# A five-branch recurrent decoder layer on one core: start, attention, C heads, S5 taps and output reordered

## What is computed

```python
h = rmsnorm(x, norm_pre)
p = split_cols(h @ w_in)                       # 2048 -> columns of the five branches
oa = s5_branch(p["a_x"], ...)                  # complex diagonal recurrence, then GLU
ob = hgrn2_branch(p["b_q"], p["b_f"], p["b_i"], ...)
oc = gla_branch(p["c_q"], p["c_k"], p["c_v"], p["c_r"], ...)   # 4 heads, values 256 wide
od = rglru_branch(p["d_x"], ...)               # width-4 conv, gated recurrence
oe = mem_attend(p["e_q"], mem_k, mem_v)        # 4 heads over 256 memory tokens
branches = stack([oa * silu(p["a_g"]), ..., oe * silu(p["e_g"])])
pb = einsum("ntcw,cwd->ntcd", branches, w_branch)
merged = einsum("ntcd,ntcd->ntd", sigmoid(h @ w_merge), pb)
y = x + rmsnorm(merged @ w_out, norm_post)
```

## Time and profile before

| | us |
|---|---|
| median of 3 runs (lowest, highest) | 2093.11 (2087.61, 2093.49) |
| the profiled execution | 2093.22 |
| its span in the trace | 2091.40 |
| TensorE busy (matmul) | 1990.5, 95% |
| TensorE weight loads busy | 1906.4, 91% |
| VectorE / ScalarE / GpSimd busy | 1278.6 / 906.3 / 411.4 |
| granted clock, mean over the span | 0.974 |

### The profile page before, as it was taken

The page is one execution under the profiler, slowest core; times in us unless marked ns, Lnnn a source line. Parts: engine busy times, 40 slices in busy tenths (PEclk is TensorE's granted clock), DMA queues, the critical chain, the costliest instruction groups (busy, mean ns, idle before and its releaser), DMA issues.

```text
span 2091.4 us, 36635 instructions
## 1 busy us (share of the span) xinstructions
PE 1990.5 (95%) x15254; PEld 1906.4 (91%) x15254; DVE 1278.6 (61%) x2092; ACT 906.3 (43%) x1307; POOL 411.4 (20%) x708
## 2 busy tenths in 40 slices
PE   6999986999999999999999999999999999999995
PEld 5889986999998989898999999999999999999994
DVE  6654437777665656565777777777565565554543
ACT  4533433444553434343555555545333333433342
POOL 3678877875000000000000000000100000000000
PEclk9999998999998989898999999999999999999997
DMA  6766754555443434444444444444655444555441
GB/s 237 256 245 243 264 181 134 174 182 187 157 159 134 160 136 151 145 149 159 139 143 153 141 150 144 147 140 137 219 165 191 161 155 149 193 178 165 151 162 66
DMA packets 91222, 350.46 MB, mean 168 GB/s; under 512 B 11728, under 2 KB 11872, under 8 KB 87472
## 3 DMA queue, kind: packets, MB, share of 16 engines
q1 hardware_dynamic: 76032, 278.17, 40.3%
q0 software_dynamic: 12144, 49.85, 6.7%
q10 hardware_dynamic: 2880, 20.09, 2.5%
HBM read 321.15 MB, written 26.92 MB: 166 GB/s over the span
## 4 chain that ended last, share of the span: by engine, by line
PE 58%; DVE 7%; ACT 4%; issue 3%; DMA 0%; POOL 0%; ACTq 0%; DVEq 0%
PE ps L1581 57%; DVE w_lo L1034 2%; DVE g_X L1028 1%; DVE g_X L1034 1%; ACT g_t L566 1%; ACT w_hi L566 1%; ACT L566 1%; DVE g_X L1037 0%; ACT g_X L566 0%; DMA a_h<-in_a_h 0%; DVE g_b L1439 0%; PE ps L1869 0%; DVE acc L1031 0%; DVE acc L1028 0%; DVE g_k L1034 0%
## 5 line engine op out<-in xcount | busy, mean ns | idle before, releaser
L1581 PE MATMUL ps<-h_hi,w_hi 128*128 128x288 f32 x2960 | 892.9, 302 | 39.6 <-DVE w_lo L1034 22.9
L1034 DVE TENSOR_TENSOR w_lo<-raw,w_hi 128x1024 fp32r<-128x1024 f32 x522 | 649.6, 1255 | 439.5 <-ACT w_hi L566 436.0
L1581 PE MATMUL ps<-h_hi,w_lo 128*128 128x288 f32 x2960 | 877.8, 297 | 0.0
L1581 PE MATMUL ps<-h_lo,w_hi 128*128 128x288 f32 x2960 | 875.4, 296 | 0.0
L566 ACT ACTIVATE w_hi<-raw 128x1024 fp32r<-128x1024 f32 x522 | 547.3, 1056 | 655.3 <-PE ps L1581 646.9
L1581 PEld LDWEIGHTS ps<-h_hi,w_hi 128*128 128x128 f32 x2960 | 559.7, 189 | 60.6 <-issue 43.0
L1581 PEld LDWEIGHTS ps<-h_hi,w_lo 128*128 128x128 f32 x2960 | 560.7, 189 | 2.3 <-issue 1.9
L1581 PEld LDWEIGHTS ps<-h_lo,w_hi 128*128 128x128 f32 x2960 | 561.7, 190 | 0.0
L1581 PE MATMUL ps<-br_hi,w_hi 128*128 128x288 f32 x640 | 196.0, 306 | 0.5 <-DVE d_gate L1040 0.5
L1581 PE MATMUL ps<-br_hi,w_lo 128*128 128x288 f32 x640 | 192.9, 301 | 0.0
L1581 PE MATMUL ps<-br_lo,w_hi 128*128 128x288 f32 x640 | 192.6, 301 | 0.0
(11 more groups left out here) (369 smaller groups left out, 2465.0 us busy)
## 6 DMA issues: line engine op xcount, KB each, us to landing
raw<-in_w SPq DMA_DIRECT2D x522, 512.0 KB, 3.8
w_scratch<-st_wide POOLq DMA_DIRECT2D x72, 128.0 KB, 3.2
a_w<-w_scratch POOLq DMA_DIRECT2D x8, 1152.0 KB, 7.6
acc<-in_kc ACTq DMA_DIRECT2D x4, 2048.0 KB, 9.3
vc<-in_vc ACTq DMA_DIRECT2D x4, 2048.0 KB, 9.4
c_S<-in_gla POOLq DMA_DIRECT2D x4, 1024.0 KB, 6.1
out_gla_s<-c_S POOLq DMA_DIRECT2D x4, 1024.0 KB, 4.2
h_S<-in_hgrn POOLq DMA_DIRECT2D x8, 512.0 KB, 3.7
```

Of the source, the lines that this page charges most:

```text
L1034: return dve.tensor_tensor(out, a, b, ALU.subtract)
L1581: return pe.matmul(out, a, b, start=start, stop=stop)
```

## The change

It makes these edits; the time of each is left to the prediction.

- **Start.** The quarter sums of squares become two additions of tiles. `eq 0` runs each quarter's eight `x_hi` products before it waits for that quarter's `split`. DVE adds the memory's squares down to two tiles a half, and PE sums them with 4 matmuls between the two units of `eq 1`.
- **E.** `ev 2i` moves ahead of the scores, and the first fill block ahead of the transposes of `vT`. The copy of the turned values (`e_vm`) stands behind the first query copy in ACT's order.
- **D's preparation.** `d_cols` and `d_sp` lie in `rstd` now and are loaded early; the decay constants are made in three steps in E's heads 0 to 2, the conv of turn 0 in head 3 before its last output, and two more units are split there ahead of it.
- **C.** The mixing of value tile 0, then `bD`, then that of tile 1, a gate block, `updates(0)`, a branch block, the sums, a gate block, `updates(1)`, a branch block; the steps of ACT and DVE follow that.
- **S5.** The taps are made in four 32-wide pairs of groups (8 matmuls of 128 columns), and `a_K` is [128, 4, 32], multiplied as four diagonal tiles of 32 x 32.
- **Output.** `out 0` waits for each `o_lo` when it comes to it. Y is finished and stored in parts of 4, 4, 4, 2, 1, 1 tiles, by SP.

The diff, cut to its core:

```diff
+Y_PARTS = ((0, 4), (4, 4), (8, 4), (12, 2), (14, 1), (15, 1))
...
-        d_cols = sb("d_cols", [P, 8, WT], F32, d_st)
-        d_sp = sb("d_sp", [P, 8, WT], F32, d_st)
+        d_cols = rstd[:, 0:64].rearrange("p (a b) -> p a b", a=8)
+        d_sp = rstd[:, 64:128].rearrange("p (a b) -> p a b", a=8)
...
+            for n, (k, width) in enumerate(Y_PARTS):
+                sp.wait_ge(S("y_ready"), n + 1)
+                sp.dma_start(t["out_y"][:, k:k + width], acc[:, k:k + width]).then_inc(S("y_stored"), 16)
+            sp.wait_ge(S("y_stored"), 16 * len(Y_PARTS))
...
-            for q in range(4):
-                ks = slice(q * KT // 4, (q + 1) * KT // 4)
-                pool.wait_ge(S("y_ready"), q + 1)
-                load(t["out_y"][:, ks], acc[:, ks], "y_stored")
             pool.wait_ge(S("a_stored"), 16)
-            pool.wait_ge(S("y_stored"), 64)
...
+            load(d_cols, t["d_cols"], "d_cols_landed")
...
+                if i == 1:
+                    act.wait_ge(S("d_abs_lam"), 1)
+                    f(d_sp[:, 0], d_sp[:, 1], ACT.Exp, "d_exp_lam", scale=-1.0)
...
+                    if v == 0:
+                        act.wait_ge(S("e_vt"), i + 1)
+                        f(vm[:], ps[:, 6].rearrange("p (a b) -> p a b", a=2), ACT.Copy, "e_vm")
...
+                else:
+                    upto(END["gE", 2] + 2)
...
-                upto(u0 + 18)
+                upto(u0 + 19)
+                gate("D", 4 * i + 1)
+                upto(u0 + 20)
                 inverse_root(i, 2)
-                upto(u0 + 20)
-                gate("D", 4 * i + 1)
-                high_outputs(i, 2, vals, br0_hi)
                 upto(u0 + 22)
                 gate("D", 4 * i + 2)
+                high_outputs(i, 2, vals, br0_hi)
...
-                sg(dve.tensor_reduce(gate_t[:, q], sq[:, q * 4:q * 4 + 4].rearrange("p k t -> p t k"), AX.X, ALU.add), "x_ksum")
+                link(add(sq[:, 4 * q:4 * q + 2], sq[:, 4 * q:4 * q + 2], sq[:, 4 * q + 2:4 * q + 4]))
+                sg(add(gate_t[:, q], sq[:, 4 * q], sq[:, 4 * q + 1]), "x_ksum")
...
-            upto(5)
+            for half in range(2):
+                k = 8 * half
+                dve.wait_ge(S("squared"), 5 + half)
+                link(add(sq_m[:, k:k + 4], sq_m[:, k:k + 4], sq_m[:, k + 4:k + 8]))
+                sg(add(sq_m[:, k:k + 2], sq_m[:, k:k + 2], sq_m[:, k + 2:k + 4]), "m_ksum")
+                upto(4 + half)
...
             sg(dve.reciprocal(st_den, st_den), "a_inverse")
+
+            def conv(i):
...
+            def decay(step):
...
+                if step == 0:
+                    dve.wait_ge(S("d_cols_landed"), 16)
+                    link(ts(d_sp[:, 2], lam, -1.0, 0.0, ALU.mult, ALU.max))
+                    link(ts(d_sp[:, 3], lam, 0.0, None, ALU.max))
+                    sg(add(d_sp[:, 1], d_sp[:, 2], d_sp[:, 3]), "d_abs_lam")
+                    sg(ts(d_sp[:, 5:7], d_cols[:, 5:7], 0.5, None, ALU.mult), "d_halved")
+                elif step == 1:
+                    dve.wait_ge(S("d_exp_lam"), 1)
...
+                        link(mul(poly, poly, z2))
+                        link(ts(poly, poly, 1.0 / odd, None, ALU.add))
...
+                    decay(i)
+                    upto(END["eg", 2 * i + 3] + 4)
                 else:
                     upto(END["gE", 2])
+                    dve.wait_ge(S("d_params"), 48)
+                    conv(0)
+                    upto(END["gE", 2] + 2)
...
 
...
+                weigh("D", 4 * i)
+                upto(u0 + 18)
                 new_states(i, 2, vals, 0)
                 own_values(i, 2, vals, 1)
-                upto(u0 + 18)
-                weigh("D", 4 * i)
-                new_states(i, 2, vals, 1)
-                outputs(i, 2, vals)
                 upto(u0 + 20)
                 weigh("D", 4 * i + 1)
+                upto(u0 + 21)
+                outputs(i, 2, vals)
+                new_states(i, 2, vals, 1)
+                upto(u0 + 23)
                 low_outputs(i, 2, vals, br0_hi, br0_lo)
-                upto(u0 + 22)
...
-                raw_taps = ps[:, 7].rearrange("p (n g c) -> p n g c", n=4, g=8)
-                link(mul(a_K[:].rearrange("p n (g c) -> p n g c", g=8), raw_taps,
-                         in_group[:].unsqueeze(1).unsqueeze(3).to_broadcast([P, 4, 8, 16])))
-                sg(stt(a_K[:, 0], ident[:], a_d[:, i:i + 1], a_K[:, 0], ALU.mult, ALU.add), "a_K")
+                if i == 0:
+                    dve.tensor_reduce(diagonal, ident[:].rearrange("p (a c) -> p c a", c=32), AX.X, ALU.add)
+                    link(dve.tensor_reduce(in_pair, in_group[:].rearrange("p (a h) -> p h a", h=2), AX.X, ALU.add))
+                raw_taps = ps[:, 7, 0:P].rearrange("p (n h c) -> p n h c", n=4, h=2)
+                link(mul(a_K[:].rearrange("p n (h c) -> p n h c", h=2), raw_taps,
+                         in_pair.unsqueeze(1).unsqueeze(3).to_broadcast([P, 4, 2, 16])))
...
+                    if u == 0 and between:
+                        between()
...
-            project(("eq", 0), h_hi, h_lo, wait_x={0: 1, 4: 2, 8: 3, 12: 4})
-            for k in range(KT):
-                if k % 8 == 0:
-                    pe.wait_ge(S("squared"), 4 + k // 8 + 1)
-                ins = mm(ps[:, 3, 0:N_MEM], ones[:], sq_m[:, k], k == 0, k == KT - 1)
-            sg(ins, "norm_summed")
-            h("eq", 1)
+            out = out_of(("eq", 0))
+            for q in range(4):
+                if q % 2 == 0:
+                    pe.wait_ge(lo_ready, q // 2 + 1)
+                pe.wait_ge(S("high"), q + 1)
+                for k in range(4 * q, 4 * q + 4):
+                    mm(out, w_hi[:, k // UK, k % UK], h_hi[:, k], k == 0, False)
+                    mm(out, w_lo[:, k // UK, k % UK], h_hi[:, k], False, False)
+                pe.wait_ge(S("split"), q + 1)
+                for k in range(4 * q, 4 * q + 4):
+                    ins = mm(out, w_hi[:, k // UK, k % UK], h_lo[:, k], False, k == KT - 1)
+                if q % 2:
+                    sg(ins, units_done)
+
+            def mem_sum():
+                for k in (0, 1, 8, 9):
+                    pe.wait_ge(S("m_ksum"), k // 8 + 1)
+                    ins = mm(ps[:, 3, 0:N_MEM], ones[:], sq_m[:, k], k == 0, k == 9)
+                sg(ins, "norm_summed")
+
+            project(("eq", 1), h_hi, h_lo, between=mem_sum)
...
                     project(("ek", 2 * i + v), m_hi, m_lo, N_MEM, wait_x={0: 5, 8: 6} if i + v == 0 else ())
+                project(("ev", 2 * i), m_hi, m_lo, N_MEM)
...
-                project(("ev", 2 * i), m_hi, m_lo, N_MEM)
                 project(("ev", 2 * i + 1), m_hi, m_lo, N_MEM)
+                project(fill[0], h_hi, h_lo)
...
                 sg(ins, "e_vt")
-                for n in range(2):
-                    project(fill[n], h_hi, h_lo)
+                project(fill[1], h_hi, h_lo)
...
-            def mixed(i, nv, vals):
+            def mixed(i, nv, vals, v):
...
+                if v == 0:
+                    w("att", 3, 3)
+                    w("cross_out")
+                    pe.wait_ge(S("g_S0_landed"), n * 16 + 16)
+                out, val = ps[:, 2 + v], lambda m: vals[2][:, m, v * P:(v + 1) * P]
...
+                    ins = mm(out[:, seq], vals[0][:, b, v * P:(v + 1) * P], g_X[:, CROSS, seq], False, b == NB - 1)
+                if v < nv - 1:
+                    return
...
                 h("cg", 2 * i + 1)
-                mixed(i, 2, c_values)
-                updates(i, 2, 0)
+                mixed(i, 2, c_values, 0)
                 if i == 0:
                     pe.wait_ge(S("d_lo"), WT)
                 branch("D", 4 * i)
+                mixed(i, 2, c_values, 1)
+                gate("D", 4 * i + 1)
+                updates(i, 2, 0)
+                branch("D", 4 * i + 1)
                 sum_squares(i, 2, c_values)
+                gate("D", 4 * i + 2)
                 updates(i, 2, 1)
-                gate("D", 4 * i + 1)
-                branch("D", 4 * i + 1)
-                gate("D", 4 * i + 2)
                 branch("D", 4 * i + 2)
                 gate("D", 4 * i + 3)
...
                 for k in range(2):
-                    ins = mm(ps[:, 7], w[:, 0, k], w[:, 4:8, k], k == 0, k == 1)
+                    for pair in range(4):
+                        own = slice(32 * pair, 32 * pair + 32)
+                        ins = mm(ps[own, 7, 0:P], w[:, 0, k, own], w[:, 4:8, k, own], k == 0, k == 1)
...
                 for n in range(BLK):
-                    mm(y[:, :, n:BLK], a_K[:, n], u[:, :, 0:BLK - n], n == 0, False)
+                    for pair in range(4):
+                        own = slice(32 * pair, 32 * pair + 32)
+                        mm(y[own, :, n:BLK], a_K[own, n], u[own, :, 0:BLK - n], n == 0, False)
...
-            pe.wait_ge(S("o_lo"), KT)
             for n in range(KT):
-                project(("out", n), o_hi, o_lo)
```

(1 more changed line is left out.)

105 lines of the change are left out of this document (47 added, 58 removed).

## The result

The changed kernel takes 2010.66 us (median of 4 runs, 2009.41 to 2014.98) against 2092.66 (4 runs, 2087.61 to 2093.49): the ratio is 0.9617 (95% interval 0.9596 to 0.9638), 82 us less. Forecast were 2012 and a range of 2003 to 2026. The profiled execution took 2009.41 us with a span of 2007.7 (before 2093.22 and 2091.40), so 83.7 us of span are gone. The sum said 81.0.

The account below looks back on a forecast made before the run. TensorE's own work was taken to set the time nearly everywhere, with losses in its waits and lower clock. Gains 6.3 + 12.1 + 21.1 + 22.2 + 6.5 + 6.3 + 6.5 = 81.0 took 2093.2 to 2012 us, range 2003 to 2026.

Parts of the forecast that it names:

- C heads: C heads: parting the two mixings by a dense block ends most low-clock time; 22.2 us gained, bounds 13.7 to 27.3.
- 3/8 x 8 x 1.7 = 5.1 us stay: C heads: 8 mixings at B's rate of clock falls, 3 of 8, 1.7 us lost each, leave 5.1 us.
- Rival (a): Mixings still bring the clock down each time: 2021 if all eight for 3.4 us, 2034 if as long as before; chance 0.15.
- E heads: Four E heads: waits for `vT` and ahead of the scores go; 12.1 us gained, bounds 8 to 12.3.
- D's preparation: Ahead of D: the 18.9 us gap and 2.2 us of low clock behind it go; 21.1 us gained, bounds 18 to 21.1.
- D's turns: D's stage after its preparation: no gain or loss of its own was predicted, 0 us.
- rival (b): Early side, E's decay step and the conv: a new wait replaces an old one, 3 + 4 + 3 us, 2022; chance 0.11.
- Start: Up to the first key block: earlier sums, shorter `eq 0`, fewer `sq_m` matmuls; 6.3 us gained, bounds 2.4 to 8.4.
- `ek 0` needs a bank that DVE frees behind `m_lo`: Start: the memory's norm moves up only some 6 us, limiting the gain to 6.3 instead of 8.4.
- S5: S5 stage: `prepare` gains 0.8 us a turn, 6.5 for eight; products with `a_K` unchanged, taken as 0.
- Rival (c): S5's products with `a_K`: the diagonal tiles don't overlap, 35 us lost, 2047; chance 0.05.
- End: Program end: POOL's 6.9 us drain is hidden with stores on SP, less 0.4; 6.5 us gained, bounds 0 to 8.

Follow-up runs that it names:

- `d_back`: The changed kernel with the decay constants and the first conv put back behind the E heads; 2029.63 us.
- `mem_back`: The changed kernel with the memory's squares summed by 16 matmuls behind the first block again; 2018.27 us.

## Why the prediction was right

The time fell for the reasons given, most of all in C and in D's preparation, but the close total hides errors of 11.0 us one way and 8.2 the other.

**C heads (22.2, measured 25.4).** The mechanism is shown, from both sides and in its two halves. The step "3/8 x 8 x 1.7 = 5.1 us stay" took B's rate of falls for C. Eight profiled executions had C in this order, the changed kernel's and seven others, and their low stretches in C number 0, 2, 0, 2, 1, 6, 0 and 5: 2.0 on average, 3.4 us of loss, where I had 3 and 5.1. The changed kernel's profiled execution drew a zero, which is luck worth 3.4 us against that mean. Rival (a), all eight each time, never came.

**E heads (12.1, measured 13.7) and D's preparation (21.1, measured 21.1).** The waits went as the prediction said, and the decay step "tight and counted at nothing" cost 0.2 us once. The other 1.6 us in E, beyond the bound of 12.3, are busy time: 231.35 us for the same 1936 matmuls instead of 233.02. Why is open. `d_back` gave the 21.1 back in the trace; E's new order had no run of its own.

**D's turns (0, measured -8.2).** This is the step that failed. The prediction priced the conv at its new place and asked whether it was in time; it did not ask what the rest of D would stand beside, 43 us earlier. POOL's arithmetic ends at about 500 us in both kernels, D's start moved from 328 to 285, and so more of its turns run beside POOL. The size fits: TensorE's waits in D's turns came to 11.6 us instead of 6.6, and two low stretches of 3.4 us cost 1.7 each. I had seen that "DVE's tiny steps took 0.35 us each there, twice what some of them took" and used it for rival (b) alone. So (b) came true in part, in D instead of E: new waits of up to 2.8 us, and 3.4 us of low clock twice. The criterion "wrong by a new PE wait over 1 us that repeats" was met by `gate_t` (two of 1.0, one of 1.6, one of 1.8), and the forecast held only because the gains of other terms had been put too low.

**Start (6.3, measured 10.0).** The failed step is "`ek 0` needs a bank that DVE frees behind `m_lo` [...] and the norm of the memory moves up less". The reciprocal did come 6.8 us earlier (37.69 against 44.48), but the step behind it came 8.9 us earlier. The kernel before shows why:

```profile
44.48 1.75 DVE L1101 RECIPROCAL rstd<-sd 128x256 f32<-128x256 f32 x1 [5.04 <-ACT sd L566]
48.39 1.22 DVE L1034 TENSOR_TENSOR w_lo<-raw,w_hi 128x1024 fp32r<-128x1024 f32 x1 [2.15 <-ACT w_hi L566]
49.53 0.87 DVE L1040 SCALAR_TENSOR_TENSOR mem<-mem,norm_cols,rstd 128x256 f32<-128x256 f32 x2
```

After the reciprocal VectorE sat idle for 2.15 us, for a weight split that waited for TensorE's units. So the normalizing was paced by the stream and not by the norm, and `mem_back` shows the same from the other side (7.07 us of matmuls on the path instead of 2.12, 5.1 us later). The bound of 8.4 was too low as well, since `eq 0` was worth more than "3.4 us in all": it ended at 31.83 us instead of 36.87, 5.0 earlier. 5.0 and 5.0 are the 10.0 measured.

**S5 (6.5, measured 7.3).** `prepare` gained 0.75 a turn, the products with `a_K` lost 0.04. The other 1.6 is a shorter wait for `half_out` (0.7 instead of 1.4) and small differences. Rival (c) is out. **Output (6.3, measured 6.3)** went as worked out; neither had a run of its own. **End (6.5, measured 8.2):** "I take nothing there, and 0.4 lost" was mis-sized. Drain 7.0, other differences between POOL's and SP's way 0.8, smaller last store 0.4 net of its additions.

## What to carry to other kernels

Read the granted clock beside the busy time: TensorE can be busy without a gap and still lose 6% of a stage, where matmuls of few columns stand together, and a 3-us dense block between them gives it back. Before moving a stage earlier, list what the other engines do at its new time, not only whether its inputs are ready. And judge a change of a few us by the stage in the trace, since falls of the clock that come and go moved the time of the C heads in one and the same order by up to 9 us.

## What was not expected of the hardware

- The same C order had between 0 and 6 low stretches of 3.4 us in eight profiled executions. What decides it in one execution is open. The two kernels with C's mixings cut had none, which is too few to tell, as three of the eight had none either.
- VectorE's elementwise steps took up to 1.9 times as long beside POOL (0.77 us against 0.41), beside its arithmetic and beside its issuing of a transfer, but not beside transfers alone. Holding POOL back took 2.0 us from TensorE's wait for `xc` and put 1.6 on a later one.
- POOL's drain took 6.9 us at the end of the program, and 14.0 us where it stood early and hidden.
- 8 matmuls of 4 columns (16 records) took 1.95 us at 1.00 and 3.58 at 0.50, and products on four diagonal 32x32 tiles took 1.56 us where those on the full array took 1.52.
